# Ten products of the identity during the load of x, and another order on PE: gate tiles, prompt scores, parameters, conv rows and the last transposes of a decoder trunk on one core

## The reference

```python
xn = rmsnorm(h, g_attn)
z = xn @ w_in          # 8 heads of q, k/v of three branches, S5 input u, merge gates gA and gB (1024 wide each)
q, k = rope(rmsnorm_heads(q)), rope(rmsnorm_heads(k))
A = attention(q, k, v, caches, head_gates) @ w_a    # prompt rows and decode rows
y, states = s5_scan(u)                              # then GELU and a GLU: B
h += (sigmoid(gA) * A + sigmoid(gB) * B) @ w_o
h += (gelu(causal_conv(gate)) * value) @ w_down     # gate, value = rmsnorm(h) @ w_up
h += sigmoid(rmsnorm(h) @ w_ple_gate) * (p @ w_ple)
```

## Time and profile before

| | us |
|---|---|
| runs | 1194.3, 1193.85, 1188.97 |
| median of the runs | 1193.85 |
| the profiled execution | 1188.44 |
| its span, first to last instruction | 1186.8 |
| PE busy in the span | 1120.9 (94%) |
| DVE, ACT, POOL busy | 482.5, 286.5, 156.4 |
| mean granted clock of PE | 0.989 |

### The profile page before, as it was taken

How to read it: one execution, slowest core, us unless ns; L and a number is a source line. 1 busy time by engine, 2 the same in 40 slices (tenths; PEclk the granted TensorE clock), 3 DMA queues, 4 the chain that set the end, 5 groups by cost and what they waited for, 6 DMA issues and landing times.

```text
span 1186.8 us, 16480 instructions
## 1 busy us (share of the span) xinstructions
PE 1120.9 (94%) x6314; PEld 921.3 (78%) x6314; DVE 482.5 (41%) x1209; ACT 286.5 (24%) x917; POOL 156.4 (13%) x276
## 2 busy tenths in 40 slices
PE   6998898899999999999999899889999999999995
PEld 4886775678888888888887777666878888888884
DVE  4989615713243222252436854372324223210031
ACT  3434324510111111210344442252112111110021
POOL 6444410002100000005003532000000000000000
PEclk9999899999999999999999999999999999999998
DMA  9553662234645553454645367322444555435430
GB/s 242 172 145 92 205 195 53 72 107 146 165 138 151 142 142 112 123 143 132 205 145 161 97 164 256 77 60 94 142 114 138 155 155 148 120 113 150 139 121 36
DMA packets 239423, 162.23 MB, mean 137 GB/s; under 512 B 25344, under 2 KB 233240, under 8 KB 239208
## 3 DMA queue, kind: packets, MB, share of 16 engines
q1 hardware_dynamic: 229858, 144.45, 42.2%
q0 software_dynamic: 4752, 14.58, 4.3%
q10 hardware_dynamic: 4736, 2.16, 0.7%
HBM read 157.94 MB, written 7.58 MB: 139 GB/s over the span
## 4 chain that ended last, share of the span: by engine, by line
PE 85%; DVE 9%; issue 2%; ACT 2%; DMA 1%; SPq 0%; ACTq 0%; POOL 0%; DVEq 0%; POOLq 0%
PE bank_act L690 39%; PE bank_dve L690 36%; DVE kT L1762 1%; PE bank_dve L1001 1%; PE bank_act L875 1%; PE bank_act L1067 1%; PE bank_o L1081 1%; DVE pcw L1769 1%; PE bank_o L1030 1%; DVE Sf L1751 1%; DVE vpast L1765 1%; DVE vpast L1759 1%; DVE Sf L1766 1%; DVE Sf L1864 0%; DVE mx L1867 0%
## 5 line engine op out<-in xcount | busy, mean ns | idle before, releaser
L690 PE MATMUL bank_act<-xn,ring 128*128 128x264 f32 x1568 | 367.2, 392 | 4.9 <-DVE xn L1727 4.4
L690 PEld LDWEIGHTS bank_act<-xn,ring 128*128 128x128 f32 x1568 | 300.1, 193 | 61.3 <-issue 8.5
L690 PE MATMUL bank_dve<-R,ring 128*128 128x264 f32 x704 | 157.6, 386 | 0.0
L690 PE MATMUL bank_dve<-xn,ring 128*128 128x264 f32 x672 | 156.4, 386 | 0.0
L690 PEld LDWEIGHTS bank_dve<-R,ring 128*128 128x128 f32 x704 | 133.4, 190 | 22.6
L690 PEld LDWEIGHTS bank_dve<-xn,ring 128*128 128x128 f32 x672 | 127.7, 190 | 21.8
L1946 DVE TENSOR_SCALAR PT<-GX,PT 128x264 f32<-128x264 f32 x44 | 18.3, 417 | 200.7 <-ACT GX L1212 200.6
L1212 ACT ACTIVATE GX<-bank_act 128x264 f32<-128x264 f32 x44 | 17.2, 391 | 269.1 <-PE bank_act L690 269.1
L1212 ACT ACTIVATE xn<-hT 128x264 f32<-128x264 f32 x32 | 13.5, 423 | 210.3 <-DVE hT L1965 149.8
L638 POOL DMA_DIRECT2D out_dram<-kall x2 | 1.0, 518 | 466.4 <-ACT kall L1212 466.4
L690 PE MATMUL bank_dve<-sg,ring 128*128 128x264 f32 x256 | 58.6, 388 | 2.9 <-DVE sg L1922 2.9
(11 more groups left out here) (371 smaller groups left out, 1380.2 us busy)
## 6 DMA issues: line engine op xcount, KB each, us to landing
ring<-in_w_up_dram SPq DMA_DIRECT2D x88, 512.0 KB, 5.1
ring<-in_w_in_dram SPq DMA_DIRECT2D x28, 1024.0 KB, 6.0
ring<-in_w_down_dram SPq DMA_DIRECT2D x32, 704.0 KB, 4.6
ring<-in_w_glu_dram SPq DMA_DIRECT2D x16, 512.0 KB, 4.3
ring<-in_w_o_dram SPq DMA_DIRECT2D x8, 1024.0 KB, 5.1
ring<-in_w_ple_gate_dram SPq DMA_DIRECT2D x8, 1024.0 KB, 5.1
PT<-in_cache_cmp_dram SPq DMA_DIRECT2D x64, 64.0 KB, 2.3
ring<-in_w_a_dram SPq DMA_DIRECT2D x8, 512.0 KB, 6.0
```

Of the source, the lines that this page charges most:

```text
L690: ins = pe.matmul(out, lhsT, rhs, start=(k == 0), stop=(k == nk - 1))
```

## The change

It moves work in the order of PE, with what ACT, DVE and SP do for it, in five places. (1) In the prologue PE multiplies the identity by itself ten times into bankO, between the landing of the identity and that of x; the parameters' transposes stand behind the fifth tile of x, DVE's and ACT's preparations are put in another order, and the sum of squares stands behind job 0. (2) Of the four gate tiles behind the S5 states two go into the job loop (behind job 14 in layer 0, behind job 5 in layer 1); the squares of q and k go from DVE to ACT (`z_squares`), and ACT takes the roots inside the job loop. (3) `head_scores(0)` goes ahead of the compressed scores; (2) and (3) stand side by side with a gate tile ahead of the decode products; in the head loop the gate tiles stand at heads 1, 5, 9 and 13, ahead of `turn_probs(u)`. (4) The conv rows' transposes go ahead of w_o's wait for the merge. (5) The epilogue takes the first four tiles of h when they are done.

```diff
-GATES_AT = (8,)
+GATES_AT = ((8, 14), (5, 8))
-SUM_AT = (1, 0)
+SUM_AT = (0, 0)
-GATES_IN_HEADS = (3, 5, 9, 13)
+GATES_IN_HEADS = (1, 5, 9, 13)
+ROOT_AT = (15, 16)
@@ PE, prologue
                 pe.wait_ge(ident_in, 32)
+                for _ in range(10):
+                    pe.matmul(bankO[:, 0:P], c_id[:], c_id[:], start=True, stop=True)
                 pe.wait_ge(x_in, 32)
                 for k in range(KD):
-                    if k == 2:
+                    if k == 5:
                         params_turned(0, dve_bank)
@@ PE, behind the transposes of the states
-                gates(4)
+                gates(2)
@@ PE, scores
+                head_scores(0)
+
                 banks = [dve_bank() for _ in range(KV)]
...
-                head_scores(0)
                 head_scores(1)
                 gates(1)
...
                 last.then_inc(act_ready, 1)
+                head_scores(2)
+                head_scores(3)
+                gates(1)
                 pe.wait_ge(v_in, L * V_LOADS + V_LOADS)
...
-                pe.wait_ge(c_prob, L + 1)
-                head_scores(2)
-                gates(1)
-                head_scores(3)
                 bank = act_bank()
@@ PE, head loop
                     if u % 4 == 0:
                         turn_cmp(u // 4)
+                    if u in GATES_IN_HEADS:
+                        gates(1)
                     turn_probs(u)
                     if u % 2 == 0 and u + 5 < 2 * H:
                         head_scores(u + 4)
                         head_scores(u + 5)
-                    if u in GATES_IN_HEADS:
-                        gates(1)
@@ PE, ahead of w_o (taken out behind i == 1)
+                pe.wait_ge(conv_in, L * 48 + 48)
+                bank = act_bank()
+                for f in range(KF):
+                    last = pe.transpose(bank[:, 20 * f:20 * f + 20], conv_rows[:, P * f:P * f + P], ident[0:20, 0:20])
+                last.then_inc(act_ready, 1)
                 pe.wait_ge(merged, L * KD + KD)
@@ PE, epilogue
-                pe.wait_ge(h_done, DEPTH * KD + KD)
-                for t in range(3):
-                    m = P if t < 2 else NB
-                    for j in range(2):
+                for j in range(2):
+                    pe.wait_ge(h_done, DEPTH * KD + 4 * j + 4)
+                    for t in range(3):
+                        m = P if t < 2 else NB
@@ ACT, job loop
+                    if jobs == 13:
+                        z_squares(0)
+                        z_squares(1)
+                    if jobs == 14:
+                        z_squares(2)
+                        if jobs in GATES_AT[L]:
+                            gates(2)
+                    if jobs == ROOT_AT[L]:
+                        act_.wait_ge(hvar_ready, L + 1)
+                        fn(ss[:, 0:2, :], ss[:, 0:2, :], ACT.Sqrt)
+                        fn(ss[0:NB, 2, :], ss[0:NB, 2, :], ACT.Sqrt).then_inc(hstd_ready, 1)
@@ DVE, prologue
+            x_tile(1)
+            x_tile(3)
             prep_steps(0)
-            for k in range(1, KD, 2):
...
-            prep_angles(0)
+            prep_params(0, 0)
+            for k in range(KD):
+                if k in (3, 6):
+                    x_tile(5 if k == 3 else 7)
...
             for k in range(KD):
                 add_squares(0, 0, k)
+            prep_angles(0)
@@ DVE, head norms
-                dve.wait_ge(act_freed, act_jobs(L, "pe", 1))
...
-                    tt(w[:, 0:QW].rearrange("p (h d) -> p h d", h=H), zq, zq, MUL)
-                    link(tt(w[:, QW:896].rearrange("p (j g d) -> p j g d", j=3, g=KV), zk, zk, MUL))
-                    link(dve.tensor_reduce(ss[0:m, t, :], w.rearrange("p (h d) -> p h d", d=HD), AX, ADD))
+                    dve.wait_ge(z_squared, L * 3 + t + 1)
+                    ins = dve.tensor_reduce(ss[0:m, t, :], z_sq[t][0:m].rearrange("p (h d) -> p h d", d=HD), AX, ADD)
```

More of the change, by code:

```diff
@@ L132, in params_taken @@
 def params_taken(L):
-    return 2 if L == 0 else dve_jobs(L - 1, "down", DOWN_PREP[0] + 1 + 1)
+    return 3 if L == 0 else dve_jobs(L - 1, "down", DOWN_PREP[0] + 1 + 1)
 def direct_taken(L):
@@ L143, in qkv_jobs @@
 def qkv_jobs(L, j):
-    return min(j + 1, JOBS) + max(0, j + 1 - LAG[L]) + 4 * (j >= U_AT) + 4 * (L == 0 and j >= B_AT[0]) + 2 * sum(g <= j for g in GATES_AT)
+    return min(j + 1, JOBS) + max(0, j + 1 - LAG[L]) + 4 * (j >= U_AT) + 4 * (L == 0 and j >= B_AT[0]) + 2 * sum(g <= j for g in GATES_AT[L])
 def caches_turned(L, s):
@@ L154, in probs_turned, with weight_chunks @@
 def probs_turned(L, u):
-    return act_jobs(L, "p_probs", u + u // 4 + 2 + sum(v < u for v in GATES_IN_HEADS))
-def weight_chunks():
+    return act_jobs(L, "p_probs", u + u // 4 + 2 + sum(v <= u for v in GATES_IN_HEADS))
+def weight_chunks(L):
     names = []
@@ L165, in weight_chunks @@
             names += [("u", j) for j in range(2)]
[L166 to L170, removed]
+        if 3 * i + 2 in GATES_AT[L]:
+            names += [("gate", GATES_AT[L].index(3 * i + 2))]
+    before_cmp = 5
+    names += [("gate", i) for i in range(len(GATES_AT[L]), before_cmp)]
     names += [("cmp", i) for i in range(2)]
@@ L183 @@
 V_LOADS = 16 * (NB * PAGES + 2)
-CHUNKS = weight_chunks()
-NCH = len(CHUNKS)
+CHUNKS = [weight_chunks(L) for L in range(DEPTH)]
+NCH = len(CHUNKS[0])
 def trunk(nc, A, C, O):
@@ L485, in slot_count @@
         def slot_count(m):
-            return sum(16 * dmas_of(n) for n, _ in (CHUNKS * DEPTH)[m % SLOTS:m + 1:SLOTS])
+            return sum(16 * dmas_of(n) for n, _ in sum(CHUNKS, [])[m % SLOTS:m + 1:SLOTS])
         @block.gpsimd
@@ L984, in layer, with head_scores @@
                     last.then_inc(dve_ready, 1)
+                def head_scores(u):
+                    c, t, g = unit(u)
+                    bank = dve_bank()
+                    n = P * (t + 1)
+                    pe.matmul(bank[:, 0:2 * n], qT[64 * g:64 * g + 64, c, P * t:P * t + P], kT[64 * g:64 * g + 64, :, 0:n],
+                              start=True, stop=True).then_inc(dve_ready, 1)
+                head_scores(0)
                 banks = [dve_bank() for _ in range(KV)]
@@ L994, in layer @@
                                 last.then_inc(dve_ready, 1)
[L996 to L1001, removed]
-                              start=True, stop=True).then_inc(dve_ready, 1)
-                head_scores(0)
                 head_scores(1)
@@ L1118, in layer @@
                     columns(256, 2, sg[:, 0], KD, dve_bank, dve_ready)
-                    if i == 1:
-                        pe.wait_ge(conv_in, L * 48 + 48)
-                        bank = act_bank()
-                        for f in range(KF):
-                            last = pe.transpose(bank[:, 20 * f:20 * f + 20], conv_rows[:, P * f:P * f + P], ident[0:20, 0:20])
-                        last.then_inc(act_ready, 1)
                     if i == 2:
@@ L1435, in _ @@
                 fn(SS[:, CMP0:KEYS], SS[:, CMP0:KEYS], ACT.Exp, bias=sq4[:, 6:7], accum_out=sq4[:, 10:11]).then_inc(s_exp, 1)
-                gates(1)
-                act_.wait_ge(c_arg, L + 1)
-                fn(SP_, SP_, ACT.Exp).then_inc(c_exp, 1)
                 def exps(u):
@@ L1447, in _ @@
                 exps(0)
+                act_.wait_ge(c_arg, L + 1)
+                fn(SP_, SP_, ACT.Exp).then_inc(c_exp, 1)
+                gates(1)
                 fn(PTs[:, 0:4 * P], take(base)[:]).then_inc(act_freed, 1)
@@ L1486, in _ @@
                         small_parameters(L + 1)
-                squares(L, 1, dve_freed, lambda k: dve_jobs(L, "w_o", k + 1), range(4))
-                fn(cvT.rearrange("p f r -> p (f r)"), take(base)[:, 0:20 * KF]).then_inc(act_freed, 1)
-                squares(L, 1, dve_freed, lambda k: dve_jobs(L, "w_o", k + 1), range(4, 6))
+                squares(L, 1, dve_freed, lambda k: dve_jobs(L, "w_o", k + 1), range(6))
                 for k in range(2):
```

86 lines of the change are left out of this document (48 added, 38 removed).

## The result

The changed kernel takes **1159.22 us** (median of 6 runs, 1157.64 to 1164.06) against 1191.57 for the kernel before (6 runs, 1186.46 to 1194.68): a ratio of **0.9737**, 95% interval 0.9709 to 0.9764. Forecast were 1165 and a range of 1152 to 1181. The profiled execution of the changed kernel took 1164.06, the slowest of its six; its span is 1162.3, 24.5 us less than the 1186.8 of before. The sum of the forecast, made for that, was 25.6.

A forecast was written before the change was run, and what follows sets the result against it. PE was taken to bound the kernel (85% of the chain), with only its waits to gain. Seven terms sum to -25.6 us: 1162.8 against the profile's 1188.4, about 1165 with the runs' offset; range 1152 to 1181.

The forecast's parts named there:

- The main reading: Whole kernel: PE bounds it, and moved work fills PE's waits; about 1165 us, chance 0.72.
- The rival that the waits only move: S5 ends and head loop: a covered wait lengthens the next, so nothing is gained there; 1179.5 us, chance 0.15.
- part 4: Decode attention and first scores: filled waits and scores side by side give -2.85 us a layer, -5.7 in two.
- Part 1: Prologue: parameters behind the fifth x tile and a new order start the first xn product earlier; -1.6 us.
- Part 2: End of layer 0's S5: two gate tiles fill 7.4 us of waits and slow clock, less 3.2 new waits; -4.2 us.
- Part 3: Layer 1's job loop: two gate tiles behind job 5 fill waits, leaving 2.4 of 6.2 us; -3.8 us.
- Parts 4 and 5: Decode attention, first scores and head loop, up to w_a: filled PE waits give -6.05 us a layer.
- The head loop's term: Head loop: gate tiles ahead of heads 1, 5, 9 and 13 cover waits for DVE; -6.4 us in two layers.
- The slower rival: Head loop: gate tiles delay DVE's chain, 14.4 us a layer, 28.8 in both; 1200 us, chance 0.04.
- Part 6: Conv rows: 22 transposes moved from w_o into the wait ahead of it; -2.9 us.
- part 7: Kernel end: three of six transpose groups fill the 1.5 us wait for h; -1.0 us.
- The drain: ACT's table loads: the skill adds some 1.38 us per switch; the forecast counted nothing, else its sum were about -20.

The follow-up runs named there:

- run 4: The changed kernel with the head loop's gate tiles back at heads 3, 5, 9 and 13, behind turn_probs and the scores: 1165.94 us.
- run 3: The changed kernel with the 22 conv-row transposes back inside w_o, behind its second chunk: 1161.80 us.
- run 7: The changed kernel with four gate tiles behind the S5 states again, none behind jobs 14 and 5; squares and roots stay on ACT: 1176.77 us.
- run 9: The changed kernel with ten more identity products ahead of xn (layer 0) and nine ahead of the pe_rows in each layer: 1158.49 us.
- run 8: The kernel before with only the S5 gate tiles moved into the job loop; DVE still squares q and k: 1195.66 us, ratio 1.0039.
- run 5: The changed kernel with the head loop's four gate tiles in pairs ahead of heads 5 and 13: 1166.16 us.
- run 6: The changed kernel with scores (2), a gate tile and scores (3) behind the decode products again: 1160.82 us.
- run 12: The changed kernel plus identity products in each layer: nine ahead of the pe_rows, four ahead of the decode scores, one ahead of the compressed scores: 1159.93 us.
- run 2: The kernel before with the ten identity products at the start alone: 1189.00 us, ratio 0.9988.

## Why the prediction was right, and where not

**The main reading** held: the gain is waits of PE, filled in place. The rival that the waits only move would have given 1179.5; undoing the head loop's places, the conv rows and the S5's tiles costs 6.2, 3.3 and 14.4 us by their stretches (runs 4, 3, 7), so these gains are real. Of the other moves, those of ACT and DVE in part 4 and the last transposes were not undone by themselves; for them the account rests on the trace.

**Part 1 (-1.6; measured -2.5).** The mechanism was right: the gains, the squares and then ACT's sine and cosine set the end. The products took 4.6 us instead of 4 and delayed x by 1.0 to 1.2 us instead of 0.5, but x was then transposed faster (0.44 instead of 0.69 us for two transposes), so that the gains ended at 14.5 instead of the 15.2 worked out; with them the start gains 2.5, without them 1.7. The wait ahead of xn and the low clock behind it stayed, as said.

**Part 2 (-4.2; measured -2.9).** The step that failed is the one that took the low clock behind the waits as gone for good (1.0 in the tiles, 0.9 in the transposes). The new wait for ACT is 2.25 us in place of the 3.2 put there, so on that the forecast was on the safe side; but the clock falls behind it, and the two tiles take 9.77 instead of 7.36 us, 2.4 more (run 9).

**Part 3 (-3.8; measured -4.7).** New waits are 1.3 us ahead of the states and some tenths, instead of the 2.4 left for them. The forecast gave the gain to the tiles, with DVE's earlier norms as a condition that it did not price. Runs 7 and 8 show that neither is worth anything in this part without the other.

**Parts 4 and 5 (-6.05 a layer; measured -6.0 and -4.5).** The head loop's term was exact (3.1 against 3.2, run 4; the waits for DVE are 3.0, forecast was "some 3"). The slower rival did not come: one tile is covered, a pair is not (run 5). That leaves 2.9 of the 6.0 of layer 0 for part 4, as forecast (2.85), but its terms are right only in sum, which is luck. The wait ahead of the decode products was credited to the gate tile with 1.2; run 6 shows some 0.2 net for it there, while the other moves, forecast at 0.6, brought about 1.7. Layer 1 gained 1.5 less because in this execution the clock was down for longer in its decode part (1.1 of it in the one tile of 6.60 us). The forecast had no term for that fall, which the kernel before has in both layers: undisturbed layers of the changed kernel take 96.5 us, 7.7 less than the 104.2 of before.

**Part 6 (-2.9; measured -3.3)** and **part 7 (-1.0; measured -0.5):** the last transposes start 0.85 us earlier, and 0.3 of it is given back behind them.

**The drain** that the Trainium skill adds to a switch of tables (ScalarE: Activation LUTs, What ACT_TABLE_LOAD costs) does not show in the trace of the changed kernel either (the load ends at 123.82, the root starts at 123.83, and the instruction ahead of the load ends at 122.53, the load starts at 122.54), and counting nothing for it was right.

**The total.** For the pair of profiled executions the sum was 1.1 us off (-25.6, -24.5). The median is 5.8 below the 1165, as the profiled execution of the changed kernel (1164.06) is its slowest of six and that of before (1188.44) lies in the faster half. Part of it are the falls of the clock in the decode part, which come in some executions and not in others (96.5 to 99.8 us for the same stretch). Where the clock fell in the unprofiled runs is not shown.

## What to carry to other kernels

Look for work that depends on little (here gate tiles, scores, small transposes) and put it into the waits of the bounding engine, one piece ahead of each wait rather than several ahead of one: a piece is free as long as the engine that is waited for has that much work in hand. Where such a piece stood as cover elsewhere, what it covered has to be made earlier in the same change, or the wait just moves behind it; neither half of such a change can be judged alone. A wait ahead of large products can cost twice, by itself and by the lower clock behind it, so ask of each new wait what runs behind it.

## What the runs showed of the hardware that was not expected

- With a wait of 2.25 us of PE between the cache rows and the gate tiles the granted clock was 0.76 on average over 14 us, and the products behind it took 2.4 us more; with the identity multiplied in the wait it was 1.00 (run 9).
- A wait is not needed for the clock to fall: from 170 to 180 us of run 12 PE was busy throughout, mostly with products on tiles smaller than 128x128, and the clock was 0.88, from 180 to 185 us 0.89. Nor do these products alone make it fall: in layer 1 of the same run it was 1.00 over them.
- Ten products at the start, some 20 us ahead of the first product with xn, made the transposes right behind them faster (0.44 against 0.69 us for two), but by the first product with xn nothing of it was left, and the kernel before with them alone is the same (ratio 0.9988).
- The granted clock of the rows does not show the slow passes at the start of the kernel before. Eight passes of 256 columns take 3.78 us in both kernels (and 1.89 later), but the clock listed over them is 1.00 before, from 16 to 19 us, and 0.50 in the changed kernel, from 13 to 16:

```profile
16.22 3.78 PE L690 MATMUL bank_act<-ring,uT 128*128 128x256 f32 x8
```

```profile
13.03 3.78 PE L695 MATMUL bank_act<-ring,uT 128*128 128x256 f32 x8
```

So mean granted clocks of two kernels need not mean the same: the profiled execution of run 2 has 0.985 at 1188.94 us, a run of the kernel before beside it 0.989 at 1188.99.
